# Two transformer blocks on one core: the first layer's last input slab in eight steps inside the attention's first units, one pair of score banks for units 0 to 4, and four convolution taps earlier

## The reference

```
u = rms_norm(h, mix_norm_g[l])
proj = u @ w_in[l]
q, k, v, glu_a, glu_g = jnp.split(proj, splits, axis=-1)
attn_out = moba_attention(heads(q), heads(k), heads(v), rel_bias)
conv_out = conformer_conv(glu_a, glu_g, conv_w[l], conv_b[l], conv_ln_g[l], conv_ln_b[l])
mixed = jnp.concatenate([attn_out, conv_out], axis=-1)
h = h + mixed @ w_out[l]
```

## Time and profile before

| | us |
|---|---|
| median of 3 runs (lowest to highest) | 1838.95 (1838.95 to 1841.34) |
| the profiled execution | 1838.65 |
| its span, first to last instruction | 1836.8 |
| PE busy in the span | 1793.2 |
| DVE busy in the span | 1095.2 |
| ACT busy in the span | 739.8 |

### The profile page before, as it was taken

One profiled execution on the slowest core, in us unless ns is written; L12 is line 12 of the kernel. 1 busy time (PEld: TensorE's weight loads), 2 busy tenths in 40 slices (PEclk: granted clock), 3 DMA queues, 4 the chain that ended last, 5 costly groups with the idle time before them and its releaser, 6 DMA issues.

```text
span 1836.8 us, 23391 instructions
## 1 busy us (share of the span) xinstructions
PE 1793.2 (98%) x8864; PEld 1445.6 (79%) x8864; DVE 1095.2 (60%) x1647; ACT 739.8 (40%) x1061; POOL 132.1 (7%) x123
## 2 busy tenths in 40 slices
PE   7999999999999999989999999999999999999998
PEld 5886788888887787768888888887855888888887
DVE  6998444444433676544766673337998367666423
ACT  4237443333323234454544442322258354445321
POOL 1000100000011110731000000100000100000000
PEclk9998999999999999999999999999999999999999
DMA  5320222322232521202232223233310222322232
GB/s 197 123 93 24 69 92 91 105 100 91 92 115 92 169 72 47 69 24 92 92 108 98 91 91 115 92 120 93 113 47 1 69 92 95 110 92 91 94 113 69
DMA packets 27687, 167.39 MB, mean 91 GB/s; under 512 B 3499, under 2 KB 5675, under 8 KB 8801
## 3 DMA queue, kind: packets, MB, share of 16 engines
q1 hardware_dynamic: 23840, 157.13, 25.1%
q0 software_dynamic: 1920, 6.42, 1.2%
q10 hardware_dynamic: 1856, 2.85, 0.6%
HBM read 161.93 MB, written 2.13 MB: 89 GB/s over the span
## 4 chain that ended last, share of the span: by engine, by line
PE 91%; DVE 6%; ACT 2%; issue 1%; DMA 0%; DVEq 0%; ACTq 0%
PE ps L435 26%; PE ps L437 26%; PE ps L436 26%; PE ps L659 2%; PE ps L611 2%; PE ps L630 2%; DVE ring L1581 1%; PE ps L448 1%; PE ps L450 1%; PE ps L449 1%; DVE ring L1573 1%; ACT ring L1063 1%; DVE score L1786 1%; DVE w_lo L1286 0%; PE ps L695 0%
## 5 line engine op out<-in xcount | busy, mean ns | idle before, releaser
L435 PE MATMUL ps<-a_hi,w_hi 128*128 128x512 f32 x1608 | 632.7, 393 | 9.6 <-DVE a_lo L1292 3.8
L436 PE MATMUL ps<-a_lo,w_hi 128*128 128x512 f32 x1608 | 626.9, 390 | 0.0
L437 PE MATMUL ps<-a_hi,w_lo 128*128 128x512 f32 x1608 | 626.8, 390 | 0.0
L435 PEld LDWEIGHTS ps<-a_hi,w_hi 128*128 128x128 f32 x1608 | 302.4, 188 | 84.1 <-issue 15.8
L436 PEld LDWEIGHTS ps<-a_lo,w_hi 128*128 128x128 f32 x1608 | 302.4, 188 | 63.5 <-issue 1.7
L437 PEld LDWEIGHTS ps<-a_hi,w_lo 128*128 128x128 f32 x1608 | 302.4, 188 | 63.4
L1286 DVE TENSOR_TENSOR w_lo<-raw,w_hi 128x2048 fp32r<-128x2048 f32 x80 | 188.1, 2352 | 216.3 <-ACT w_hi L872 215.9
L872 ACT CAST w_hi<-raw 128x2048 fp32r<-128x2048 f32 x79 | 150.3, 1902 | 300.0 <-PE ps L437 259.7
L435 PE MATMUL ps<-h_hi,w_hi 128*128 128x512 f32 x516 | 200.7, 389 | 0.0
L436 PE MATMUL ps<-h_lo,w_hi 128*128 128x512 f32 x516 | 200.7, 389 | 0.0
L437 PE MATMUL ps<-h_hi,w_lo 128*128 128x512 f32 x516 | 200.7, 389 | 0.0
(11 more groups left out here) (248 smaller groups left out, 2004.1 us busy)
## 6 DMA issues: line engine op xcount, KB each, us to landing
raw<-weights_dram SPq DMA_DIRECT2D x146, 1024.0 KB, 4.8
bias_t<-bias_rows_scratch POOLq DMA_DIRECT2D x8, 256.0 KB, 4.8
ncb<-decay_rows_scratch POOLq DMA_DIRECT2D x8, 256.0 KB, 5.0
xT<-x_in_dram ACTq DMA_DIRECT2D x4, 256.0 KB, 5.2
xT<-x_in_dram SPq DMA_DIRECT2D x4, 256.0 KB, 4.7
raw<-weights_dram SPq DMA_DIRECT2D x2, 512.0 KB, 7.9
out_dram<-xT SPq DMA_DIRECT2D x4, 256.0 KB, 2.1
v<-pT POOLq DMA_DIRECT2D x1, 1016.0 KB, 6.7
```

What stands on the lines that cost most here:

```text
L435: pe.matmul(dst, wh, hi[:, k0 + k, :], start=start and k == 0, stop=False)
L436: pe.matmul(dst, wh, lo[:, k0 + k, :], start=False, stop=False)
L437: last = pe.matmul(dst, wl, hi[:, k0 + k, :], start=False, stop=stop and k == nk - 1)
```

## The change

The last slab of the input projection no longer stands in a row with the others. PE's loop over slabs ends at slab 8, and slab 9 is issued as eight steps of 12 products behind the scores of units 0, 1 and 2 (three, three and two steps). Since it writes banks 2 and 3, the first five units all use banks 0 and 1. ACT copies slab 9 out in step 0 of the attention, and casts slab 11 in step 2; DVE splits slab 11 in step 3. The table of taps has two more behind slab 0 and two more behind slab 1. DVE's own loop still counts ten slabs.

```
+STEPS1 = {-3: [(9, 0), (9, 1), (9, 2)], -2: [(9, 3), (9, 4), (9, 5)], -1: [(9, 6), (9, 7)]}
+ALONE1 = 5
...
-            return u.t == 2 and u.n < ALONE or u.t == 3 and u.n < ALONE3
+            return u.n < {1: ALONE1, 2: ALONE, 3: ALONE3}[u.t]
...
-                if u.t == 1 and u.n < 2:
-                    wait("qkv", 5 + u.n)
+                if u.t == 1 and u.n in (0, ALONE1):
+                    wait("qkv", 5 if u.n == 0 else 6)
...
+                if u.t == 1 and u.n == 8:
+                    wait("qkv", 6)
...
-                    wait("qkv", QKV[name] + j)
+                    wait("qkv", 4 if name == "in1" else QKV[name] + j)
...
-            for j in range(10):
+            for j in range(9):
...
-            attend(runs_of(1)[0])
+            attend(runs_of(1)[0], STEPS1)
...
+            def last_values(i):
+                if i == 0:
+                    wait("slab", BASE["in1"] + 10)
+                    A.copy(v1[:, :, 256:512], ps[:, 2:4, :].rearrange("p b (t c) -> p (b t) c", c=256)
+                           ).then_inc(sem["qkv"], 1)
+                elif i == 2:
+                    split(BASE["out1"] + 1)
...
-            attend(runs_of(1)[0], spare=lambda i: split(BASE["out1"] + 1) if i == -1 else None)
+            attend(runs_of(1)[0], spare=last_values)
...
-                    taps(7)
+                    taps(9)
...
-                    taps(10 if j < 4 else 9)
+                    taps(12 if j == 1 else 10 if j < 4 else 9)
...
-                if i == 0:
+                if i == 3:
                     split(BASE["out1"] + 1)
```

More of the change, by code:

```diff
@@ L1169, in _ @@
                     A.activation(tmp[:, 0, :], ps[:, 2 * (o % 2) + 1, :], ACT.Sigmoid).then_inc(sem["glu_g"], 1)
-                if j < 9:
-                    split(n + 2)
+                split(n + 2)
                 if j >= 4:
@@ L1178, in _ @@
                     else:
-                        A.copy(v1[:, :, 256 * (j - 8):256 * (j - 7)], bank.rearrange(
-                            "p b (t c) -> p (b t) c", c=256)).then_inc(sem["qkv"], 1)
+                        A.copy(v1[:, :, 0:256], bank.rearrange("p b (t c) -> p (b t) c", c=256)
+                               ).then_inc(sem["qkv"], 1)
[3 more added lines that the diff above has]
+                    A.copy(v1[:, :, 256:512], ps[:, 2:4, :].rearrange("p b (t c) -> p (b t) c", c=256)
+                           ).then_inc(sem["qkv"], 1)
+                elif i == 2:
+                    split(BASE["out1"] + 1)
             act.preload_act_table_set("natural_log_exp_and_others")
-            attend(runs_of(1)[0], spare=lambda i: split(BASE["out1"] + 1) if i == -1 else None)
+            attend(runs_of(1)[0], spare=last_values)
             for c in range(4):
@@ L1490, in _ @@
             tap_order, latest = [], {}
-            for hi, n in ((1, 7), (2, 12), (3, 12), (4, 4 * TAPS - 31)):
+            for hi, n in ((1, 9), (2, 14), (3, 12), (4, 4 * TAPS - 35)):
                 for _ in range(n):
```

## The result

The changed kernel takes 1844.12 us (median of 8 runs, 1843.92 to 1846.22), the kernel before 1838.84 in the same rounds (8 runs, 1837.69 to 1841.34). The ratio is 1.0033, with a 95% interval of 1.0024 to 1.0042: slower, by 5.3 us between the medians (the ratio makes 6.1). The profiled execution of the changed kernel took 1846.22, 2.1 above its median and the slowest of the eight, so a total is read from the medians and a place from the rows. About 1 us of the difference between the two profiled executions arises in the second layer's drain, which the change does not touch. At the end of the first layer's attention the rows are 6.3 us apart.

What follows compares the result with a forecast made beforehand. TensorE, busy 98% of the span, bounds the kernel, with VectorE's queue setting the pace in the attention's fill. +4.4 at the last read, -0.8 drain, +1.7 clock make +5.3 on 1838.65: 1844.0 us, range 1839.5 to 1848.5.

Steps and rivals of the forecast that it cites:

- The walk: First layer's attention, unit by unit: DVE's reads come later, +4.6 at unit 4, +6.4 after unit 7, +4.4 at the last.
- the sum: Whole kernel: +4.4 at the last read, -0.8 in the drain, +1.7 for the fill's clock, together +5.3 us.
- the places that were named as signs: Rows of the changed kernel: DVE reads unit 7 near 155.5 to 157.5 and the last near 173 to 175.
- the clock in the fill: Attention's fill, after PE's wait ahead of unit 1: half-clock time costs +1.7 us, with ends of 0 and +3.4.
- The drain: After DVE's last read: the slow-clock stretch may not come, between 0 and -1.7 us, taken as -0.8.
- The price: Fill of the attention: the taps ahead of DVE's first read of scores cost the time, not sharing banks itself.
- The four taps: Moved ahead of unit 0, 2.65 us: delay DVE's first read by 1.1; three give 2.0 back before the last read.
- The moved split: DVE's split of slab 11 (2.20 us) now follows unit 6, so +4.6 becomes +6.8 at unit 7.
- Covered and faster: Rival: unit 1's scores start at 127.9, PE's 3.9 us of idle time in the fill goes, 1834.7 us; 10%.
- Mostly caught up: Rival: fill's clock stays at 1.00, drain loses its slow stretch, slack absorbs delay; 1840 to 1841.5 us; 22%.
- The clock falls twice: Rival: a second slow stretch near units 4 and 7, the drain's stays; 4.4 + 3.4 + 1.7 = +9.5, 1848.2 us; 12%.

Runs made afterwards that it cites:

- sharing-only kernel: The kernel before with only the banks changed: units 0 to 4 share one pair, slab 9 in one row, taps as before; 1840.68 us against 1838.12, ratio 1.0010.
- the copy first: The changed kernel with ScalarE's copy of slab 8's v put ahead of its cast of slab 10; 1845.73 us, ratio 1.0036 to the kernel before.
- the taps back: The changed kernel with the four taps put back behind unit 0, eight steps and shared banks kept; 1843.10 us, ratio 1.0030 to the kernel before.

## Why the prediction was right

**Where PE waits.** 2.9 us ahead of unit 0 were predicted and 3.40 measured; for DVE ahead of unit 1, 6.2 and 4.06. The end of the second, 134.1, was met within 0.2 (133.94), because DVE's first read sets it (133.6 predicted, 133.37 measured). Only PE's way there was wrong: steps 0 to 2 ran at half clock and took until 129.9, not 127.9. That cost nothing, since PE would have waited.

**The walk.** Unit 3's read was put at 143.8 and the clock's +1.7, 145.5: 145.64. Unit 4's at 146.6 + 1.7 = 148.3: 148.39. Unit 7's at 148.85 + 6.4 + 1.7 = 156.95: 158.05, because the third fall of the clock, at unit 5, made DVE wait 1.00 for PE at unit 6. So the last read, 174.4 by the sum, came at 175.79. Both lie past the places that were named as signs, 155.5 to 157.5 and 173 to 175.

**The mis-sized term** is the clock in the fill: one fall that matters was charged, at +1.7, and two mattered. The fall in steps 3 to 5 made unit 3's read 1.8 late on the walk at full clock (145.64 against 143.8), and the one at unit 5 another 1.1 at unit 7, so that the last read came 7.5 late where 4.4 + 1.7 = 6.1 was charged. The drain, charged at -0.8 and measured at 7.14 - 8.33 = -1.2, made up only 0.4 of these 1.4. So the walk ends at +6.3 in the rows, 1.0 over the sum, while the medians are 5.3 apart, as the sum has it. The rows are those of the slowest of eight executions, and whether the others have the fall at unit 5 is not shown. That the medians agree with the sum to 0.1 us is luck, since executions of one kernel differ by 2 us.

**The price.** The prediction put it on the taps ahead of DVE's first read and not on sharing itself. Taking the twelve taps from ahead of that read gives back 5.4 us, all of the loss. Sharing alone does cost some 2 us, but in a row without steps, and there through the clock. The Trainium skill's page "PSUM — Partial Sum Buffer" (Summary: rules for kernel authors) wants a matmul and a reader on different banks. The trace agrees in that, with one pair, PE waits for DVE's reads at all four units of the sharing-only kernel, 3.93 us against 0.78 before (0.16 and 0.62); units 2 and 3 of the changed kernel, which begin without a wait, show that work between the units covers this once DVE has read.

**The four taps** were charged +1.1 at the first read with three of four given back at the end. Alone they are worth -3.0 us, of which the clock in the drain is 1.2; inside the changed kernel nothing that can be told. So steps and shared banks cost 5.3 + 3.0 = 8.3 us on top of the taps, but only 4.4 without them (1843.10 against 1838.67): the parts do not add up.

**The moved split.** The prediction had it add about 2.2 us to DVE's queue before unit 7. It does: DVE's part moved behind the last read gives back 3.3 us, more than its own 2.2.

**The rivals.** "Covered and faster", 1834.7, needed DVE to read early. With that the kernel reached 1838.71, not 1834.7; in its rows PE's wait of 3.40 for ACT and the half clock behind it stay, and the split is still in the queue. With the split late it came to 1835.95. A kernel that also has ACT's copy first, without a cast in the drain, was not run. "Mostly caught up" did not come: the delay of DVE's reads was 9.2 us at unit 8 (160.79 against 151.60) and at unit 12 (170.51 against 161.31), and only the taps no longer there took 1.7 off it behind that. "The clock falls twice": it fell three times in the fill, and two of these cost DVE's reads 1.8 and 1.1, 2.9 together, where 3.4 + 1.7 was priced; the fall in the drain, which this rival let stay, did not come, and the drain became 1.2 shorter.

## What to carry to other kernels

Work put between two units fills a wait only if the engine that frees their buffers gets to them in time; look first at what stands in that engine's queue, and move that. A side job of another engine, here a cast of 1.9 us, stood better in this pipeline where several units were in flight than in its fill or drain, where it held up the one copy that PE needed next. And a wait that looks covered can still be paid in clock, so read the granted clock of the stretch behind it.

## What the runs showed of the hardware

Short waits did not have the same effect each time. Ahead of unit 1 a wait of 4.06 us was followed, 1.1 us after its end, by a granted clock of 0.50 and one of 3.23 by 1.00; in the drain a wait of 1.80 was followed by 0.50 in the kernel before and by 1.00 in the changed kernel with the taps back. In the sharing-only kernel the clock fell at 134, behind two waits of 1.17 and 0.86. The Trainium skill's page "TensorE: Matmul & The Clock Gate" (HAM oscillation — how this bites in real kernels) names a wait between bursts of matmuls as what lets the clock fall. The rows bear that out in part: the falls told of here stand in or behind a wait, but not every wait has one behind it (3.23 and 1.80), and what decides it stays open here.

A wait for several engines can be named wrongly: 2.41 us put down to DVE's `ring` stayed at 2.41 when DVE's split was taken away, and went to 0.61 when ACT's cast was.

Time at half clock is not always time lost. The changed kernel and the kernel before each spent 10.2 us at 0.50 in this stretch, yet the fall in steps 0 to 2 cost nothing: with the copy first these steps ran at 1.00, and PE left its wait for DVE at 134.05, against 133.94.
